# Loading x first and filling TensorE's wait with products of zeros at the start of an encoder block

## The reference

```python
n = rms_norm(h, norm1_g)
p = n @ w_in                       # 1024 x 1536: qA | kA | vA | qB | kB | vB
qa = rope(rms_norm(qa, qn_g)) * scale ; ka = rope(rms_norm(ka, kn_g))
oa = softmax(qa @ ka.T) @ va                           # 8 heads, 2 key heads
ob = softmax([qb @ kb.T + bias, sink])[..., :-1] @ vb  # |i-j| <= 128
h = h + concat(rms_norm(oa, gnorm_a), rms_norm(ob, gnorm_b)) @ w_o
h = h + hier_moe(rms_norm(h, norm2_g), ...)            # 4 groups x 8 experts, 2 per token
out = rms_norm(h, final_g)
```

## Time and profile before

| | us |
|---|---|
| median of 3 runs | 638.72 |
| lowest, highest | 636.98, 640.76 |
| profiled execution, span from first to last instruction | 639.8 |
| input product starts | 14.71 |
| first maxima start | 50.18 |
| first probability transposes start | 55.60 |

### The profile page before, as it was taken

One profiled execution on the slowest core, in us unless ns is written; L12 is line 12 of the kernel. 1 busy time (PEld: TensorE's weight loads), 2 busy tenths in 40 slices (PEclk: granted clock), 3 DMA queues, 4 the chain that ended last, 5 costly groups with the idle time before them and its releaser, 6 DMA issues.

```text
span 639.8 us, 6965 instructions
## 1 busy us (share of the span) xinstructions
PE 593.8 (93%) x2801; PEld 288.1 (45%) x2801; DVE 149.8 (23%) x331; ACT 77.6 (12%) x151; POOL 28.5 (4%) x60
## 2 busy tenths in 40 slices
PE   4999899959999999999999999999999999999984
PEld 2445657546535353544434343434353535344321
DVE  1006545251111111121213031211111111212023
ACT  2013323121000010101000101010000101010002
POOL 2031200210000000000000000000000000000001
PEclk9999989978999999999999999999999999999999
DMA  6995680073989999999999999999999999979701
GB/s 259 338 425 226 248 288 1 34 296 130 385 349 419 416 413 410 411 421 416 419 413 418 411 419 420 414 420 417 417 415 419 421 410 410 410 296 392 307 1 67
DMA packets 35939, 217.50 MB, mean 340 GB/s; under 512 B 5136, under 2 KB 6184, under 8 KB 28368
## 3 DMA queue, kind: packets, MB, share of 16 engines
q1 hardware_dynamic: 31680, 214.30, 82.3%
q10 hardware_dynamic: 4240, 2.94, 1.4%
HBM read 216.16 MB, written 1.06 MB: 340 GB/s over the span
## 4 chain that ended last, share of the span: by engine, by line
PE 91%; DVE 5%; issue 2%; DMA 1%; SPq 0%; ACT 0%; POOLq 0%; POOL 0%; DVEq 0%; ACTq 0%
PE bank L1188 33%; PE bank L1216 17%; PE bank L1175 10%; PE bank L1226 10%; PE bank L1003 7%; PE bank L1072 4%; PE bank L1062 2%; PE bank L1267 2%; DVE region_x L882 2%; PE bank L986 2%; PE bank L1040 1%; PE bank L1282 1%; PE bank L1051 1%; DMA ring<-in_norm_g_dram 1%; DVE region_q L886 1%
## 5 line engine op out<-in xcount | busy, mean ns | idle before, releaser
L1188 PE MATMUL bank<-ring,region_x 128*64 128x512 f32 x960 | 212.1, 594 | 0.6 <-issue 0.6
L1188 PEld LDWEIGHTS bank<-ring,region_x 128*64 128x64 f32 x960 | 75.0, 137 | 132.5 <-issue 132.5
L1216 PE MATMUL bank<-ring,region_q 128*64 128x512 f32 x480 | 106.3, 594 | 15.3 <-DVE region_q L886 8.7
L897 DVE TENSOR_TENSOR h<-h,bank 128x512 f32<-128x512 f32 x64 | 44.0, 687 | 238.2 <-PE bank L1226 238.2
L1216 PEld LDWEIGHTS bank<-ring,region_q 128*64 128x64 f32 x480 | 39.7, 137 | 72.2 <-issue 72.2
L1175 PEld LDWEIGHTS bank<-region_q,region_t 128*128 128x128 f32 x512 | 61.0, 199 | 14.0 <-issue 14.0
L1175 PE MATMUL bank<-region_q,region_t 128*128 128x128 f32 x512 | 64.0, 285 | 1.7 <-DVE region_q L878 1.7
L1226 PE MATMUL bank<-region_x,region_q 128*128 128x512 f32 x128 | 62.2, 618 | 0.7 <-ACT region_x L621 0.7
L1003 PE MATMUL bank<-ring,region_x 128*128 128x512 f32 x96 | 44.7, 622 | 0.8 <-DVE region_x L660 0.8
L1226 PEld LDWEIGHTS bank<-region_x,region_q 128*128 128x128 f32 x128 | 20.4, 188 | 42.4 <-DVE h L897 21.0
L621 ACT ACTIVATE region_x<-bank 128x512 f32<-128x512 f32 x32 | 19.1, 597 | 159.3 <-PE bank L1216 140.3
(11 more groups left out here) (156 smaller groups left out, 273.5 us busy)
## 6 DMA issues: line engine op xcount, KB each, us to landing
ring<-in_w_gate_dram SPq DMA_DIRECT2D x30, 2048.0 KB, 12.3
ring<-in_w_up_dram SPq DMA_DIRECT2D x29, 2048.0 KB, 12.2
ring<-in_w_down_dram SPq DMA_DIRECT2D x29, 2048.0 KB, 11.9
ring<-in_w_in_dram SPq DMA_DIRECT2D x8, 768.0 KB, 9.1
ring<-in_w_up_dram SPq DMA_DIRECT2D x12, 512.0 KB, 9.7
ring<-in_w_down_dram SPq DMA_DIRECT2D x12, 512.0 KB, 9.2
ring<-in_w_o_dram SPq DMA_DIRECT2D x2, 2048.0 KB, 8.6
ring<-in_w_gate_dram SPq DMA_DIRECT2D x8, 512.0 KB, 7.8
```

The costliest lines, as they stand in the source:

```text
L897: dve.tensor_tensor(part, part, ps[SC0 + k % 2][:], ALU.add).then_inc(sc_free, 1)
L1188: last = pe.matmul(ps[bank][64 * a:64 * a + 64, :], xgT[:, c, 64 * a:64 * a + 64], slots[s][:, c * F:(c + 1) * F], start=(c == 0), stop=(c ...
L1216: last = pe.matmul(ps[GD0 + half][64 * a:64 * a + 64, :], hT[:, c, 64 * a:64 * a + 64], w[:, c * D + 512 * half:c * D + 512 * half + 512], ...
```

## The change

SP issues x first, then all of w_in, w_o and the first expert matrices without a wait between them. ACT issues the identity (64 KB of the constants), norm1's gains in rows of their own, the one-hot table, `rel_bias` and the other gains; it squares x ahead of the copy of the bias line; the rest of the constants and the gains of q and k come behind the squares, the sinks and the router's biases behind the store of the bias line. DVE fills 512 columns with zeros, and TensorE multiplies them five times (128 x 256) into a bank that the product later starts afresh. The gains are turned in two parts, and the product for the bias line and the second of these turns stand inside the input product, behind chunk 1. On POOL the reciprocal root comes ahead of the line's memsets.

```diff
-        gain_rows = early[0:24, 3840:3968]
+        gain1_rows = early[0:8, 3840:3968]
+        gain_rows = early[0:16, 3968:4096]
...
         def _(sp):
-            sp.dma_start(cst[:], consts).then_inc(consts_in, 16)
             for t, arrived in enumerate((x_in, x1_in)):
                 sp.dma_start(h[:, t, :], x_t[t]).then_inc(arrived, 16)
-            sp.dma_start(gain_rows[0:8, :], norm1_g.rearrange("l (c p) -> (l c) p", p=P)).then_inc(gain_in, 16)
...
             for c in range(KC):
-                if c == 3:
-                    sp.wait_ge(line_stored, 16)
-                if c == 7:
-                    sp.wait_ge(bias_in, 16)
                 sp.dma_start(w_in_sb[:, c, :], w_in_c[c]).then_inc(w_in_in[c], 16)
...
             link(pool.memset(weight, 0.0))
-            pool.wait_ge(line_cut, 1)
-            pool.memset(line_sb[:, 0:2 * P - 1 - WINDOW], NEG)
-            pool.memset(line_sb[:, 2 * P + WINDOW:4 * P], NEG).then_inc(line_masked, 1)
             pool.wait_ge(ssx_ready, 2)
...
             pool.tensor_scalar(rstd1_8, rstd1, HD ** -0.5, None, ALU.mult).then_inc(rstd1_ready, 1)
+            pool.wait_ge(line_cut, 1)
+            pool.memset(line_sb[:, 0:2 * P - 1 - WINDOW], NEG)
+            pool.memset(line_sb[:, 2 * P + WINDOW:4 * P], NEG).then_inc(line_masked, 1)
...
         def _(act):
+            act.dma_start(ident, consts[:, C_ID:C_ID + P]).then_inc(ident_in, 16)
+            act.dma_start(gain1_rows, norm1_g.rearrange("l (c p) -> (l c) p", p=P)).then_inc(gain1_in, 16)
             act.dma_start(onehot_sb, onehot).then_inc(onehot_in, 16)
             act.dma_start(relb_sb, rel_bias).then_inc(onehot_in, 16)
+            act.dma_start(gain_rows[0:4, :], gnorm_a.rearrange("l (c p) -> (l c) p", p=P)).then_inc(gain_in, 16)
+            act.dma_start(gain_rows[4:8, :], gnorm_b.rearrange("l (c p) -> (l c) p", p=P)).then_inc(gain_in, 16)
+            act.dma_start(gain_rows[8:16, :], norm2_g.rearrange("l (c p) -> (l c) p", p=P)).then_inc(gain_in, 16)
...
+            act.dma_start(cst[:, P:C_ALL], consts[:, P:C_ALL]).then_inc(consts_in, 16)
             act.dma_start(gains[:, 0, :], qn_g[0].partition_broadcast(P)).then_inc(small_in, 16)
             act.dma_start(gains[:, 1, :], kn_g[0].partition_broadcast(P)).then_inc(small_in, 16)
+            act.wait_ge(line_ready, 1)
+            act.activation(line_sb, ps[7][0:8, :], ACT.Copy).then_inc(line_cut, 1)
+            act.wait_ge(line_masked, 1)
+            act.dma_start(bias_line, line_sb).then_inc(line_stored, 16)
             act.dma_start(sink_b[:], sink[0].partition_broadcast(P)).then_inc(router_in, 16)
             act.dma_start(router_b[:, 0:4], b_group[0].partition_broadcast(P)).then_inc(router_in, 16)
             act.dma_start(router_b[:, 4:36], b_expert[0].partition_broadcast(P)).then_inc(router_in, 16)
...
         def _(dve):
+            dve.memset(region_s[:, 0:512], 0.0).then_inc(zeros_ready, 1)
             dve.wait_ge(gains_turned, 1)
-            link(dve.tensor_copy(gT[:], ps[6][:, 0:24]))
+            link(dve.tensor_copy(gT[:, 0:8], ps[3][:, 0:8]))
...
+            dve.wait_ge(gains_turned, 2)
+            link(dve.tensor_copy(gT[:, 8:24], ps[6][:, 0:16]))
...
         def _(pe):
-            pe.wait_ge(onehot_in, 32)
-            pe.matmul(ps[7][0:8, :], relb_sb, onehot_sb, start=True, stop=True).then_inc(line_ready, 1)
-            pe.wait_ge(consts_in, 16)
-            pe.wait_ge(gain_in, 16 * 4)
-            pe.transpose(ps[6][:, 0:24], gain_rows[0:24, :], ident[0:24, 0:24]).then_inc(gains_turned, 1)
+            zeros = region_s[:, 0:512]
+            pe.wait_ge(zeros_ready, 1)
+            for _ in range(5):
+                pe.matmul(ps[0][:, 0:256], zeros[:, 0:P], zeros[:, 256:512], start=True, stop=True)
...
+            pe.wait_ge(ident_in, 16)
+            pe.wait_ge(gain1_in, 16)
+            pe.transpose(ps[3][:, 0:8], gain1_rows, ident[0:8, 0:8]).then_inc(gains_turned, 1)
...
             pe.wait_ge(x1_in, 16)
-            pe.wait_ge(line_cut, 1)
-            pe.wait_ge(xT_ready, 1)
...
                 last = qkv(0, QB, c, 2)
+                if c == 1:
+                    pe.wait_ge(onehot_in, 32)
+                    pe.matmul(ps[7][0:8, :], relb_sb, onehot_sb, start=True, stop=True).then_inc(line_ready, 1)
+                    pe.wait_ge(gain_in, 16 * 3)
+                    pe.transpose(ps[6][:, 0:16], gain_rows, ident[0:16, 0:16]).then_inc(gains_turned, 1)
```

More of the change, by code:

```diff
@@ L258, in build_encoder @@
         dve_chain, pool_chain = sem("dve_chain"), sem("pool_chain")
+        ident_in, gain1_in, zeros_ready = sem("ident_in"), sem("gain1_in"), sem("zeros_ready")
         pick_ready, gathered, picks_turned, xg_act, xg_dve = map(sem, ("pick_ready", "gathered", "picks_turned", "xg_act", "xg_dve"))
@@ L278, in _ @@
         def _(sp):
-            sp.dma_start(cst[:], consts).then_inc(consts_in, 16)
             for t, arrived in enumerate((x_in, x1_in)):
                 sp.dma_start(h[:, t, :], x_t[t]).then_inc(arrived, 16)
-            sp.dma_start(gain_rows[0:8, :], norm1_g.rearrange("l (c p) -> (l c) p", p=P)).then_inc(gain_in, 16)
-            sp.dma_start(gain_rows[8:12, :], gnorm_a.rearrange("l (c p) -> (l c) p", p=P)).then_inc(gain_in, 16)
-            sp.dma_start(gain_rows[12:16, :], gnorm_b.rearrange("l (c p) -> (l c) p", p=P)).then_inc(gain_in, 16)
-            sp.dma_start(gain_rows[16:24, :], norm2_g.rearrange("l (c p) -> (l c) p", p=P)).then_inc(gain_in, 16)
             for c in range(KC):
-                if c == 3:
-                    sp.wait_ge(line_stored, 16)
-                if c == 7:
-                    sp.wait_ge(bias_in, 16)
                 sp.dma_start(w_in_sb[:, c, :], w_in_c[c]).then_inc(w_in_in[c], 16)
@@ L325, in _ @@
                         sp.wait_ge(k_roped, 1)
-                        sp.wait_ge(gains_turned, 1)
+                        sp.wait_ge(gains_turned, 2)
                         sp.dma_start(w_o_sb[:, 0:4, :], w_o_c[:, 0:4, :]).then_inc(slot_in[3], 16)
@@ L482, in _ @@
         def _(act):
+            act.dma_start(ident, consts[:, C_ID:C_ID + P]).then_inc(ident_in, 16)
+            act.dma_start(gain1_rows, norm1_g.rearrange("l (c p) -> (l c) p", p=P)).then_inc(gain1_in, 16)
             act.dma_start(onehot_sb, onehot).then_inc(onehot_in, 16)
             act.dma_start(relb_sb, rel_bias).then_inc(onehot_in, 16)
+            act.dma_start(gain_rows[0:4, :], gnorm_a.rearrange("l (c p) -> (l c) p", p=P)).then_inc(gain_in, 16)
+            act.dma_start(gain_rows[4:8, :], gnorm_b.rearrange("l (c p) -> (l c) p", p=P)).then_inc(gain_in, 16)
+            act.dma_start(gain_rows[8:16, :], norm2_g.rearrange("l (c p) -> (l c) p", p=P)).then_inc(gain_in, 16)
+            act.wait_ge(x_in, 16)
+            act.activation(junk, h[:, 0, :], ACT.Square, accum_out=ssx[:, 0:1]).then_inc(ssx_ready, 1)
+            act.wait_ge(x1_in, 16)
+            act.wait_ge(ssx_ready, 1)
+            act.activation(junk, h[:, 1, :], ACT.Square, accum_out=ssx[:, 1:2]).then_inc(ssx_ready, 1)
+            act.dma_start(cst[:, P:C_ALL], consts[:, P:C_ALL]).then_inc(consts_in, 16)
             act.dma_start(gains[:, 0, :], qn_g[0].partition_broadcast(P)).then_inc(small_in, 16)
             act.dma_start(gains[:, 1, :], kn_g[0].partition_broadcast(P)).then_inc(small_in, 16)
+            act.wait_ge(line_ready, 1)
+            act.activation(line_sb, ps[7][0:8, :], ACT.Copy).then_inc(line_cut, 1)
+            act.wait_ge(line_masked, 1)
+            act.dma_start(bias_line, line_sb).then_inc(line_stored, 16)
             act.dma_start(sink_b[:], sink[0].partition_broadcast(P)).then_inc(router_in, 16)
@@ L489, in _ @@
             act.dma_start(router_b[:, 4:36], b_expert[0].partition_broadcast(P)).then_inc(router_in, 16)
[L492 to L500, removed]
             act.wait_ge(line_stored, 16)
@@ L653, in link @@
                 dve.wait_ge(dve_chain, n[0])
+            dve.memset(region_s[:, 0:512], 0.0).then_inc(zeros_ready, 1)
             dve.wait_ge(gains_turned, 1)
-            link(dve.tensor_copy(gT[:], ps[6][:, 0:24]))
[L657 to L662, removed]
+            link(dve.tensor_copy(gT[:, 0:8], ps[3][:, 0:8]))
+            for k, (t, b) in enumerate(((0, 0), (0, 1), (1, 0), (1, 1))):
+                dve.wait_ge(x_turned, k + 1)
+                dve.tensor_tensor(xT[:, 4 * b:4 * b + 4, t * P:(t + 1) * P],
+                                  ps[4 + 2 * t + b][:].rearrange("p (c t) -> p c t", c=4),
+                                  bcast(gT[:, 4 * b:4 * b + 4], 2, P), ALU.mult).then_inc(xT_ready, 1)
+            dve.wait_ge(gains_turned, 2)
+            link(dve.tensor_copy(gT[:, 8:24], ps[6][:, 0:16]))
             dve.wait_ge(k_squared, 1)
@@ L798, in _ @@
             dve.tensor_copy(hTr[:, 4:8, P:2 * P], ps[7][:].rearrange("p (c t) -> p c t", c=4)).then_inc(hTr_dve, 1)
+            dve.wait_ge(consts_in, 16)
             dve.wait_ge(rstd2_ready, 2)
```

## The result

| | before | changed |
|---|---|---|
| median of 20 runs, us | 639.85 | 644.29 |
| lowest, highest | 636.98, 643.24 | 640.59, 647.86 |
| ratio to before, 95% interval | | 1.0058 (1.0036 to 1.0080) |
| span of the profiled execution | 639.8 | 645.3 |

The change makes the kernel slower by 0.6%. (The ratio of the two medians in the table would be 1.0069; the one with the interval is not worked out from them.) The forecast was 641.4 with a range of 635.0 to 644.5, so the time lies within, 0.2 us under the upper end. Of the 2.9 us between 641.4 and 644.29, 1.15 come from the starting point: the median of before, then 638.7 from three runs, is 639.85 from twenty. The measured difference of the medians is 4.4 us, the forecast was 2.7.

A forecast was written before the change was run, and what follows sets the result against it. TensorE was taken to bound the kernel, 91% of the chain; with the bias landing last, +0.2 us at L1051 and +2.5 for a lower clock on 638.7 gave 641.4 us, range 635 to 644.5.

The forecast's parts named there:

- The head's gain: Kernel start: TensorE ready for the first probability transposes (L1051) 2.8 to 7.1 us earlier, at 48.5 to 52.8.
- The bias lands last: Bias read on ACT's queue: lands behind the whole load backlog, at 52.0 us, between 50.9 and 53.1.
- the plain count of bytes: Bias landing estimated by adding start, x, w_in, w_o, matrices, bias, small loads and landing times: 50.9 us.
- Turn by turn: DMA engines shared by two queues: they alternate packet for packet whatever the size, 0.63 us per 16 KB packet, 0.07 per bias packet.
- L1051 at 55.8: First probability transposes: start after bias, maxima and exponentials at 55.8 us instead of 55.60, +0.2.
- The clock falls, 2.5 us: TensorE after idling ahead of L1051: lower clock slows transposes by 0.9, scores 2.08 instead of 1.13, next product by 0.6.
- The sum: Whole kernel: +0.2 for L1051 and +2.5 for the clock make +2.7, 641.4 us.
- 0.30: Whole kernel: chance of being slower by over 0.5%, from the late clock and the forecast's upper end.
- the 0.53: Whole kernel: chance that the time stays within 0.5% of before.
- the late clock of that rival: TensorE behind the bias wait: clock returns late, from 6.0 us of lower-level work; +0.2 + 4.1, 643.0 us; chance 0.25.
- The rival that had the bias in time: Bias read: lands early enough that the head's gain of 2.8 to 7.1 us reaches the end, 635.9 to 631.6; chance 0.18.

The follow-up runs named there:

- one-zero kernel: Changed kernel plus SP's wait for the bias ahead of w_o, with one product of zeros instead of five: 635.76 us, ratio 0.9907 to the kernel before.
- the smaller packets: Changed kernel with the first four expert matrices loaded in four column pieces each, 4 KB packets instead of 16 KB: 632.06 us, ratio 0.9887 to the kernel before.
- the halved backlog: Changed kernel with SP waiting for the bias ahead of the two up matrices: 633.90 us, ratio 0.9899 to the kernel before.
- the one with more zeros: Changed kernel with 19 more products of zeros on TensorE ahead of the wait for the first probabilities: 641.72 us, ratio 1.0017 to the kernel before.
- the version with the wait: Changed kernel with SP waiting for the bias behind w_in's last chunk, ahead of w_o and the expert matrices: 632.33 us, ratio 0.9886 to the kernel before.

## Why the prediction was right

By its own steps:

- **The head's gain.** 2.8 to 7.1 us were expected at the point before L1051; it was 6.8, the case in which the clock is full from the product's start. Zeros end at 5.5 (said 5.7), the product starts at 8.94 (9.0 to 10.8). The one-zero kernel shows 2.2 to 3.2 us of it to be the clock.
- **The bias lands last.** Said: first packets from 22, as the last of the backlog, at 52.0, with 50.9 and 53.1 as ends. The read was issued at 20.74 and its first packets moved at 25.2, behind the three small loads on ACT's queue; when the 16 KB packets began, at 28.75, only some 260 of its 1024 pieces had gone, 16 per engine, so 48 were left for 32 turns, where the prediction had at least 37. The later start changed nothing, since the bias came last either way. It landed at 53.63, 1.6 us late and just past the upper end. Against the plain count of bytes (50.9) it is 2.7 late. The queues' packets until 60 us show where most of that lies:

```profile
q1 hardware_dynamic: 2544, 17.83, 73.1%
q10 hardware_dynamic: 2208, 2.12, 10.4%
```

That is 43.9 and 6.2 us per engine, where the sum had 42.6 (x, w_in, w_o, matrices) and 5.5 (bias and small loads): 2.0 us too little. Besides, behind w_in's first chunks the DMA engines dropped for a moment (from 14.0 to 15.4 us 198 GB/s instead of 405, a loss of 0.7 us, part of which may lie in the 2.0; what caused it stays open), and the start was slower (75 GB/s until 3.0 instead of 90, 0.1 us).

- **Turn by turn.** The count of packets (512 to 511), the smaller packets and the halved backlog all bear it out. The rule of the Trainium skill (DMA: Bandwidth & Descriptors, "Queues, rings and completion order") holds in its first half, turns by packet. Its 9 to 17 descriptors in one do not: a load's 16 KB row and a 1.5 KB piece of the bias were each a turn of their own. Equal counts over 20 us don't show that by themselves, since turns of ten against ten would give them too. Shorter windows do: one row and one piece take an engine 0.62 + 0.07 us, and in five successive windows of 0.68 us from 30.0 on the 16 engines moved 16, 15, 16, 16 and 16 packets of q1 against 16, 15, 16, 15 and 16 of q10 (in the second window one engine was on a packet of a third queue). Ten pieces of the bias in a row would take an engine 0.7 us, and the counts would jump from window to window.
- **L1051 at 55.8.** Measured 57.56. The bias explains 1.7 us of the 1.76.
- **The clock falls, 2.5 us.** Measured between the second L1059 of the changed kernel and of the one with more zeros: 2.5. The prediction's parts were 0.9, 0.95 and 0.6; measured 0.88, 0.95 and 0.71.
- **The sum.** +0.2 + 2.5 = +2.7 was the forecast for this place; measured +4.45 in the trace. The term that was too small is the landing of the bias. The remaining 1.0 us of the span's 5.5 is the later stretch at half clock: from 77.6 to 84.4 before, here from 80.0 to 90.2:

```profile
80.00:90.20 10.20, 9.49 (x38) 7.96 (x39) 7.39 (x18) 4.18 (x12) 3.17 (x4) 0.50 0.97 362
```

In both kernels it comes around the same 2.15 us of idle time, and its length differs from execution to execution; the runs of the changed kernel lie in groups at about 641, 644 and 647 us with mean granted clocks of 0.981, 0.977 and 0.972.

- **The chances.** The measured ratio, slower by 0.58%, is on the far side of the 0.5% line, where 0.30 lay, and not with the 0.53. It isn't the late clock of that rival (from L1059 on the clock was low for 5.3 us, until 62.9, under its 6.0), but the forecast's own mechanism with a later bias. That the time still lies in the range owes something to luck: the range was drawn for the late clock and for other stretches at half clock, not for a bias past 53.1, and 1.15 us of the miss are the median of before. The rival that had the bias in time is in effect the version with the wait. Its first probability transposes come 5.9 us earlier, within the 2.8 to 7.1; its whole gain, 7.3 us by the ratio, is above them; in its trace the rest is the missing later stretch at half clock.

## What to carry to other kernels

A wait on a DMA-issuing engine can be the only thing that keeps a late, finely cut load out of the company of large ones. Before taking it out, count how many of the load's pieces are left on each DMA engine when the big packets begin, and multiply by the time of one big packet (0.62 us for 16 KB here), since two queues take turns packet by packet; if more pieces are left than big packets, the load lands last of all. And after an earlier start, read which wait now ends last: here 6.8 us of head start became 9.3 us of idle time and a lower clock, and one wait put in the right place gave it all back.

## What the runs showed of the hardware that I had not expected

- Products of zeros raise the granted clock like others: but for one 8 x 8 transpose of 0.22 us they are all that TensorE had done when sixteen transposes took 1.97 us instead of 4.01. No row of before showed this.
- Small packets take a whole turn too: 48 of q1's 512 from 30 to 50 us were under 512 bytes, and q10 still moved 511.
- Loading the same 8 MB in rows of 4 KB instead of 16 KB, as strided pieces, cost nothing in time (632.06 against 632.33 us with the wait) and made the other queue's read three times as fast while they shared.
